# The low weight parts of all output projections, made by VectorE alone instead of VectorE and GpSimd in turn

## What is computed

```
h = x
# first block: one layer
h = h + mixer(rmsnorm(h))          # ends in concatenate([o, y]) @ w_out          (1024 x 1024)
h = h + cross_attn(rmsnorm(h))     # ends in o @ w_xo                             (1024 x 1024)
h = h + swiglu(rmsnorm(h))         # (silu(hn @ w_gate) * (hn @ w_up)) @ w_down
h = rmsnorm(h)
# second block: two layers
h = h + sb_moba_mixer(rmsnorm(h))  # ends in o @ ab_w_out                         (1024 x 1024)
h = h + memory_attn(rmsnorm(h))    # ends in o @ xa_w_out[0]                      (256 x 1024)
h = h + conv_ffn(rmsnorm(h))
h = h + fox_mixer(rmsnorm(h))      # ends in o @ fox_w_out                        (1024 x 1024)
h = h + memory_attn(rmsnorm(h))    # ends in o @ xa_w_out[1]                      (256 x 1024)
h = h + conv_ffn(rmsnorm(h))
return rmsnorm(h)
```

## Time and profile before

| | |
|---|---|
| time, median of 3 runs | 1246.49 us (1245.15 to 1246.93) |
| the profiled execution | 1246.37 us, of which its span is 1243.9 us |
| PE busy | 1190.4 us, 96% of the span |
| PEld busy | 1115.5 us, 90% |
| DVE busy | 809.4 us, 65% |
| ACT busy | 656.9 us, 53% |
| POOL busy | 260.3 us, 21% |
| low parts by DVE (L1681) | 216, 1231 ns each on average |
| low parts by POOL (L2495) | 97, 2431 ns each on average |
| high parts by ACT (L1126) | 313, 1050 ns each on average |
| chain that ended last | PE 82%, DVE 9%, ACT 5%, issue 3%, POOL 1% |

### The profile page before, as it was taken

One profiled execution on the slowest core, in us unless ns is written; L12 is line 12 of the kernel. 1 busy time (PEld: TensorE's weight loads), 2 busy tenths in 40 slices (PEclk: granted clock), 3 DMA queues, 4 the chain that ended last, 5 costly groups with the idle time before them and its releaser, 6 DMA issues.

```text
span 1243.9 us, 24084 instructions
## 1 busy us (share of the span) xinstructions
PE 1190.4 (96%) x9808; PEld 1115.5 (90%) x9808; DVE 809.4 (65%) x1428; ACT 656.9 (53%) x1128; POOL 260.3 (21%) x170
## 2 busy tenths in 40 slices
PE   7999999899999999999998999999999988999997
PEld 6888779898999999988896899999889867999997
DVE  4887755664644554567866676776664566776776
ACT  3443734654644444555557555555655556555554
POOL 4030000021222323221121223232212111223231
PEclk9999999899999999999999999999999999999999
DMA  8443423352565665543442456655443332655551
GB/s 318 133 125 119 131 87 120 113 177 68 184 198 182 183 187 173 170 133 106 131 135 89 151 181 179 190 182 187 140 136 119 128 123 86 194 180 186 185 174 49
DMA packets 51516, 187.54 MB, mean 151 GB/s; under 512 B 5712, under 2 KB 5840, under 8 KB 51024
## 3 DMA queue, kind: packets, MB, share of 16 engines
q1 hardware_dynamic: 51408, 186.02, 47.3%
HBM read 184.95 MB, written 1.05 MB: 150 GB/s over the span
## 4 chain that ended last, share of the span: by engine, by line
PE 82%; DVE 9%; ACT 5%; issue 3%; POOL 1%; DMA 0%; DVEq 0%; SPq 0%; ACTq 0%
PE banks L420 63%; PE banks L450 7%; ACT w_hi L1126 2%; DVE w_lo L1681 2%; PE banks L493 2%; PE banks L923 1%; PE banks L937 1%; POOL w_lo L2495 1%; DVE gates L2100 1%; DVE h L2110 1%; PE banks L903 1%; PE banks L840 1%; PE banks L817 1%; PE banks L478 1%; PE banks L1054 1%
## 5 line engine op out<-in xcount | busy, mean ns | idle before, releaser
L420 PE MATMUL banks<-a_hi,w_hi 128*128 128x256 f32 x1432 | 411.2, 287 | 6.4 <-DVE a_lo L1693 2.9
L1126 ACT ACTIVATE w_hi<-w_raw 128x1024 fp32r<-128x1024 f32 x313 | 328.5, 1050 | 158.7 <-PE banks L420 158.6
L2495 POOL TENSOR_TENSOR w_lo<-w_raw,w_hi 128x1024 fp32r<-128x1024 f32 x97 | 235.8, 2431 | 832.3 <-ACT w_hi L1126 832.3
L420 PE MATMUL banks<-a_lo,w_hi 128*128 128x256 f32 x1432 | 405.1, 283 | 0.0
L420 PE MATMUL banks<-a_hi,w_lo 128*128 128x256 f32 x1432 | 405.0, 283 | 0.0
L1681 DVE TENSOR_TENSOR w_lo<-w_raw,w_hi 128x1024 fp32r<-128x1024 f32 x216 | 266.0, 1231 | 74.3 <-ACT w_hi L1126 74.0
L420 PEld LDWEIGHTS banks<-a_hi,w_hi 128*128 128x128 f32 x1432 | 274.5, 192 | 10.5 <-DVE a_lo L1693 4.6
L420 PEld LDWEIGHTS banks<-a_lo,w_hi 128*128 128x128 f32 x1432 | 274.6, 192 | 0.4
L420 PEld LDWEIGHTS banks<-a_hi,w_lo 128*128 128x128 f32 x1432 | 274.6, 192 | 0.0
L420 PE MATMUL banks<-b_hi,w_hi 128*128 128x256 f32 x880 | 255.1, 290 | 18.9 <-DVE h L2110 3.9
L420 PE MATMUL banks<-b_lo,w_hi 128*128 128x256 f32 x880 | 250.1, 284 | 0.0
(11 more groups left out here) (383 smaller groups left out, 1318.4 us busy)
## 6 DMA issues: line engine op xcount, KB each, us to landing
w_raw<-in_weights SPq DMA_DIRECT2D x342, 512.0 KB, 3.5
h<-in_x SPq DMA_DIRECT2D x1, 1024.0 KB, 5.1
arena<-in_mem SPq DMA_DIRECT2D x1, 1024.0 KB, 12.3
early<-in_mem SPq DMA_DIRECT2D x1, 1024.0 KB, 14.3
out_h<-h SPq DMA_DIRECT2D x4, 256.0 KB, 2.6
cons<-in_cons SPq DMA_DIRECT2D x1, 546.0 KB, 7.6
arena<-in_late SPq DMA_DIRECT2D x1, 448.0 KB, 4.2
pars<-in_pars SPq DMA_DIRECT2D x1, 290.5 KB, 2.9
```

What stands on the lines that cost most here:

```text
L420: ins = mm(out, l, r, start=start and n == 0, stop=stop and n == 2, skip_group_check=check)
L1126: do(WHI[:, n % SPLIT_SLOTS, :], RAW[:, n % RAW_SLOTS, :], ACT.Copy).then_inc(*inc("w_hi_made", ("w_hi", n)))
L2495: g.tensor_tensor(WLO[:, n % SPLIT_SLOTS, :], RAW[:, n % RAW_SLOTS, :], WHI[:, n % SPLIT_SLOTS, :].bitcast(F32), ALU.subtract).then_inc(*i ...
```

## The change

`lo_on_pool` gets three lines ahead of its last rules. They say "no" for each slot of the six products; `8 * SHAPE[name][0] // 8` is the number of slots, 8 or 2.

```diff
     if s < FIRST["w_out"] + 2:
         return False
+    for name in ("w_out", "x_o", "ab_o", "m_o0", "fox_o", "m_o1"):
+        if FIRST[name] <= s < FIRST[name] + 8 * SHAPE[name][0] // 8:
+            return False
     for name in ("ffn0", "ffn1", "ffn2"):
```

## The result

| | before | changed |
|---|---|---|
| median of 5 runs each | 1246.49 us (1245.09 to 1248.56) | **1250.73 us** (1249.57 to 1251.50) |
| ratio | | 1.0036, 95% interval 1.0026 to 1.0047 |
| the profiled execution, its span | 1246.37 us, 1243.9 us | 1251.50 us, 1249.7 us |

A forecast was written before the change was run, and what follows sets the result against it. PE was taken to bound the kernel, except at four products' ends, bound by a closed DVE-ACT loop. Terms 1.11 + 1.16 + 1.23 + 1.1 = 4.6 us on 1246.4 gave 1251.0 us, range 1247.8 to 1254.5.

The forecast's parts named there:

- What bounds the kernel, and the turn: PE bounds except at ends of K = 8 residual products; there a closed DVE-ACT turn takes 3.38 us against PE's 2.88.
- The four low parts ahead of the products: Slots 63, 162, 171, 264, where DVE waits anyway: cost nothing, or 0.1 us each if that cover is short.
- The eight in the steps: Low parts inside the four products' steps: two steps of about 6.0 to 6.4 us become two closed turns, 6.76 us.
- all four terms: Later ends of the four products: w_out 1.11 us, x_o 1.16, ab_o 1.23, fox_o 1.1.
- the mean of the sums: The 28 sums of squares on DVE: mean falls from 733 ns to near 0.49 us, only slot 273's still held.
- Does it reach the end: Behind the products: each term carried in full; PE's a_lo wait at w_out's end grows from 0.30 to at least 1.4 us.
- The relief: Rival, in the steps: POOL no longer holds DVE, outweighing 9.8 us of new work; 3.2 to 7.3 us faster; chance 0.08.
- The advice to move elementwise work: Skill's rule that elementwise work belongs on VectorE, GpSimd taking about twice as long; by it ab_o would gain 1.4 us.
- The clock: Rival, behind the four ends: longer PE waits lower the granted clock, 2 us each at one or two; 1253.0 to 1255.0; chance 0.10.

The follow-up runs named there:

- square_late: Changed kernel, with ScalarE making the square of tile m after the high part of slot m + 3 in the four K = 8 products: 1242.54 us, ratio 0.9971.
- hi_early: Changed kernel, with ScalarE making slot m + 3's high part once TensorE has done slot m, in the four K = 8 products: 1233.18 us, ratio 0.9895.
- ahead4: Kernel before, with only the four low parts ahead of the products (slots 63, 162, 171, 264) moved from GpSimd to VectorE: 1246.04 us, ratio 1.0003.
- no_lock: Kernel before, with GpSimd writing zeros by memset instead of subtracting for the eight slots inside the steps: 1240.40 us, ratio 0.9967.
- all_pool: Kernel before, with GpSimd making the low parts of slots 2 to 7 in the four K = 8 products, 24 instead of 8: 1240.02 us, ratio 0.9962.
- before_again: Kernel before, unchanged, run once more for a second profile: the four products took 87.98 us, the stretch behind ab_o 20.16 us.
- hi_early_pool: Kernel before, with ScalarE's early high part alone, GpSimd keeping its low parts: 1234.10 us, ratio 0.9913.

## Why the prediction was right

**What bounds the kernel, and the turn.** Right. The turn was read as 3.38 us from six rows of one step, and the changed kernel shows 3.39. square_late shortened it by what was taken out, and hi_early opened it and let PE bound the steps at the 2.88 us that the chain had given.

**The four low parts ahead of the products.** Costed at nothing; ahead4 measured nothing (1.0003).

**The eight in the steps.** Each product was forecast from its first addition and a count of turns, and all four terms came within 0.2 us. x_o was put 0.13 too low, since its first turn takes 3.46 us and the others 3.39; fox_o 0.2 too high, since POOL's last instruction held only an a_lo and no longer the sum ahead of it. For the same reason the mean of the sums fell to 418 ns, not to the 490 forecast.

**Does it reach the end.** Right. The stages between keep their length, but for the scatter behind ab_o, and PE's wait for a_lo at w_out's end is 1.50 us where at least 1.4 was forecast. The measured 4.2 us has an interval from 3.2 to 5.9, so the time alone bears out the sign and the rough size; that the mechanism gives 4.6 is shown by the additions.

**The relief.** The sum carried it inside the terms, for the steps of before contain the holds. By itself it exists: no_lock took away holds and the products fell by 5.8 us. The Trainium skill, "SBUF — State Buffer", section "SBUF: two separate sides", is borne out by the runs on what it states of the port (2.62 us instead of 0.41 for a sum beside POOL's subtraction, 0.42 beside the memset), yet it does not give the sign of the change. What the change pays for it, the closed turns, comes to 92.96 - 82.38 = 10.6 us, by the four products of the changed kernel and of no_lock. The rival set the relief against DVE's 9.8 us of new work. That is close to the price in size, but it is not what is paid: the price is a wait, and in hi_early it went away without any work being moved.

**The advice to move elementwise work.** The advice of the Trainium skill ("GPSIMD Engine Reference", section "Engine selection") is right on the durations, 2.42 against 1.22 us. Here all_pool did the opposite of it and was faster by 10.8 us than the changed kernel.

**The clock.** Given 0.10 as a consequence of the longer waits. It falls behind ab_o and fox_o also in kernels that have no longer wait there (before_again: 0.92 behind ab_o, 0.85 behind fox_o), so most of it is a scatter on all of them and not the change's. The one fall right behind the longer wait, in the first profile of the changed kernel, looks like what this rival described, but it came at one of the eight such ends of that kernel's two profiles; whether the change makes it likelier was neither shown nor excluded. The stretch behind ab_o (2.5 us more), less the 1.1 us by which w_out began earlier, is why the first profiled span grew by 5.8 us, against 4.2 of the medians.

## What to carry to other kernels

Before work goes to the engine that does it faster, ask what stands behind it in that engine's queue and what it must wait for there: a low part that waits for a producer blocks the addition on which that same producer waits, and the turn of both, not the busy time of either, becomes the step. To find such a loop, follow one step through two timelines and add the distances from start to start; if the sum exceeds what the bounding engine needs for the step, take an operation out of the turn (put it behind what the other waits for, or issue that earlier). Here these two lines of order were worth 17.6 us (14.3 of them in the four products), where the choice of engine that this change made was worth 4.2, and nothing that could be told once the loop was open.

## What the runs showed of the hardware

A GpSimd instruction that reads two inputs from SBUF held DVE's operations with two SBUF inputs (a sum of squares took 2.62 us instead of 0.41, a low part 2.13 instead of 1.23), but not the addition to `h`, which reads a bank: in hi_early_pool it took 0.42 us in the middle of such an instruction (630.07 us, rows above). In all_pool 24 such instructions of 2.4 to 2.5 us stood in the steps of four products and held 20 a_lo there (1.45 to 1.74 us in place of 0.48), and the kernel was still faster than before, by 5 us: most of these holds lay in time for which DVE waited for PE otherwise. GpSimd's memset of the same tile, which reads nothing, shows as 0.95 us and let the sum of squares beside it run in 0.42 us.

The granted clock behind the same product differed between executions of one program: 1.00 and 0.92 behind ab_o in the two profiles of before, with 18.61 and 20.16 us for the same work. The difference of 1.55 us is over a third of what the change costs.
